# A hybrid of state space, mLSTM and differential attention on one core: one gate laid out turned, products with zeros and unread ones left out, GpSimd's order in the chunk loop, and the weight columns in one transfer

## The reference

```python
h = rmsnorm(x) * ab_norm_g
proj = h @ ab_w_in[i]            # z_a, xbc, dt_raw, z_b, q, k, v, ig, fg, og
y_a = _ssd(xbc, dt_raw, z_a, ...)        # conv, silu, scan over chunks with a state per group
y_b = _mlstm(q, k, v, ig, fg, og, z_b, ...)   # conv, silu, scan with a memory per head
y = concat([y_a, y_b]) @ ab_w_out[i]
# in _ssd:    y = (y_diag + y_off + xs * d_skip) * silu(z);  return rms(y) * norm_g
# in _mlstm:  h = rms(h * sigmoid(o_raw)) * norm_g;          return h * silu(z)
```

## Time and profile before

| | |
|---|---|
| median of 3 runs | 1576.92 us (1575.18 to 1577.39) |
| the profiled execution, its own time | 1573.38 us |
| its span | 1571.6 us |
| TensorE busy | 1525.6 us (97%) |
| VectorE busy | 907.6 us (58%) |
| ScalarE busy | 649.0 us (41%) |
| GpSimd busy | 566.1 us (36%) |
| mean granted clock of TensorE | 0.992 |

### The profile page before, as it was taken

One profiled execution on the slowest core, in us unless ns is written; L12 is line 12 of the kernel. 1 busy time (PEld: TensorE's weight loads), 2 busy tenths in 40 slices (PEclk: granted clock), 3 DMA queues, 4 the chain that ended last, 5 costly groups with the idle time before them and its releaser, 6 DMA issues.

```text
span 1571.6 us, 23657 instructions
## 1 busy us (share of the span) xinstructions
PE 1525.6 (97%) x9114; PEld 1314.0 (84%) x9114; DVE 907.6 (58%) x1484; ACT 649.0 (41%) x1272; POOL 566.1 (36%) x325
## 2 busy tenths in 40 slices
PE   8999999999999999999999999999999999999897
PEld 7798989898999987877788877888888888787686
DVE  7675878684843469999344272345544245554623
ACT  6542534353532233444345252345555333556321
POOL 3245454545344346567565330132212013211110
PEclk9999999999999999999999999999999999999899
DMA  5133333333334345765675330122111112113612
GB/s 178 41 122 94 122 94 121 94 121 94 121 108 135 100 160 186 227 199 175 220 267 201 121 94 14 28 61 76 53 54 34 34 28 80 54 35 114 254 67 107
DMA packets 151085, 176.43 MB, mean 112 GB/s; under 512 B 9671, under 2 KB 126659, under 8 KB 149955
## 3 DMA queue, kind: packets, MB, share of 16 engines
q1 hardware_dynamic: 150810, 174.92, 34.2%
q10 hardware_dynamic: 168, 0.06, 0.0%
HBM read 122.46 MB, written 52.43 MB: 111 GB/s over the span
## 4 chain that ended last, share of the span: by engine, by line
PE 47%; DVE 1%; ACT 1%; issue 1%; DMA 1%; POOL 0%; SPq 0%; POOLq 0%; ACTq 0%; DVEq 0%
PE b_ps L2404 22%; PE b_ps L2449 4%; PE b_ps L2424 4%; PE b_ps L2354 3%; PE b_ps L2356 3%; PE b_ps L2355 3%; PE b_ps L2436 2%; PE b_ps L2506 2%; PE b_ps L2507 2%; PE b_ps L2508 2%; PE b_ps L2457 1%; PE b_ps L2372 0%; DMA b_yy<-z 0%; DMA z<-b_y_T 0%; ACT a_aT L2056 0%
## 5 line engine op out<-in xcount | busy, mean ns | idle before, releaser
L1925 POOL TENSOR_TENSOR b_w<-b_w_raw,b_w 128x1024 fp32r<-128x1024 f32 x66 | 158.4, 2400 | 357.5 <-DVE b_w L2184 253.6
L2404 PE MATMUL b_ps<-a_h_hi,b_w 128*128 128x512 f32 x768 | 265.7, 406 | 2.9 <-DVE a_h_lo L2162 2.9
L393 POOL TENSOR_TENSOR b_w<-b_y_T,b_w 128x1024 fp32r<-128x1024 f32 x54 | 141.1, 2615 | 189.7 <-ACT b_w L451 189.7
L2404 PEld LDWEIGHTS b_ps<-a_h_hi,b_w 128*128 128x128 f32 x768 | 145.0, 189 | 37.1 <-issue 3.9
L2404 PE MATMUL b_ps<-a_h_lo,b_w 128*128 128x512 f32 x384 | 150.6, 392 | 0.0
L941 PE MATMUL b_ps<-b_w,p_hi 128*128 128x256 f32 x768 | 139.2, 283 | 0.0
L700 DVE SCALAR_TENSOR_TENSOR b_w_raw<-p_out_raw,p_cols,b_w_raw 128x1024 f32<-128x1024 f32 x60 | 119.8, 2003 | 12.8 <-ACT b_w_raw L482 11.4
L941 PEld LDWEIGHTS b_ps<-b_w,p_hi 128*128 128x128 f32 x768 | 120.1, 192 | 0.6
L941 PE MATMUL b_ps<-b_w,p_lo 128*128 128x256 f32 x384 | 108.7, 283 | 0.0
L2195 DVE CUSTOM_DVE_ANT_0 b_y_T<-b_ps,a_neg_dist 128x128 f32<-128x128 f32 (+5 forms) x96 | 72.1, 777 | 63.3 <-PE b_ps L2424 52.7
L451 ACT CAST b_w<-b_y_T 128x1024 fp32r<-128x1024 f32 x60 | 62.7, 1045 | 106.5 <-DVE b_y_T L661 55.0
(11 more groups left out here) (417 smaller groups left out, 3616.6 us busy)
## 6 DMA issues: line engine op xcount, KB each, us to landing
b_y_T<-in_ab_w_in SPq DMA_DIRECT2D x33, 512.0 KB, 4.3
tok<-p_out_raw SPq DMA_DIRECT2D x64, 256.0 KB, 2.3
b_w_raw<-in_ab_w_out SPq DMA_DIRECT2D x32, 512.0 KB, 3.7
b_w_raw<-in_c_w_in SPq DMA_DIRECT2D x32, 512.0 KB, 4.1
feat<-b_w_raw SPq DMA_DIRECT2D x20, 512.0 KB, 2.7
c_fe<-feat SPq DMA_DIRECT2D x7, 1280.0 KB, 6.6
yt<-b_y_T SPq DMA_DIRECT2D x8, 1024.0 KB, 10.9
b_y_raw<-yt SPq DMA_DIRECT2D x32, 256.0 KB, 3.9
```

The costliest lines, as they stand in the source:

```text
L393: gp.tensor_tensor(w_lo[s % SLOTS][:, :, :], operand(n, split_of(n, p))[:, :, :], w_hi[s % SLOTS][:, :, :].bitcast(F32), ALU.subtract).the ...
L1925: gp.tensor_tensor(w_lo[:, w, :], w_raw[u % W_RAW][:, :], w_hi[:, w, :].bitcast(F32), ALU.subtract).then_inc(S["l_wlo"], 1)
L2404: mm = pe.matmul(o, x, y, start=(k == 0 and q == 0), stop=(k == KT - 1 and q == 2))
```

## The change

- **Gate turned.** The two token blocks that make z_b (blocks 5 and 7) are computed like feature blocks and stored as features x tokens in a new tensor `zt0`; tok0 has three parts left. After the silu ScalarE multiplies by the norm's gains of the mLSTM. In the scan a chunk's cells of this gate come with a transfer of their own (`load_gate_cells`), and VectorE's copy of the turned y_b multiplies by them. What is left of L1628, the multiplication by the root, goes to ScalarE (`memory_norm`) ahead of the decays.
- **Zeros.** Chunk 0 has no products with the memory and state, no `qs` and no decay of the state; what was added to zeros is copied. The memsets of state and memory go.
- **Unread.** Chunk 7 forms no new memory and state, nor what serves them alone (`xe`, `kg`, keys turned, the state's decay).
- **Order.** `e_end` goes from VectorE to GpSimd; GpSimd's power for y_b goes ahead of its two operations on y_a; next tables ahead of the memory update; waits are split by head and by bank. In the last chunk the splits for the mid products come earlier, on GpSimd and on VectorE, which takes the low parts of units 2 and 3.
- **Columns.** The small vectors come as one matrix `columns` of 128 partitions x 140, laid out by the host (a reordering, and d_skip repeated over the partitions). The transposes and copies of rows at the start of the projection and of the scan go.
- In the projection `sum_weights(n, "T4")` moves ahead of two steps of VectorE.

```diff
-                if kinds[n] == "f":
+                if kinds[n] == "f" or gate_turned(n):
...
+            def gains_of_quarter(n, i, k):
+                if not gate_turned(n):
+                    return
+                c0 = tok_blocks[number[n]][3]
+                for b in (0, 1):
+                    gained[0] += 1
+                    act.wait_ge(S["silu_z"], gained[0])
+                    gain = CELL_GAIN + c0 + 2 * k + b
+                    nc.scalar.activation(area(i, k, b), area(i, k, b), ACT.Copy, scale=cols[:, gain:gain + 1]
+                                         ).then_inc(S["a_out"], 1)
...
+                    if kinds[n] == "t" and k == 2:
+                        gains_of_quarter(n, 0, 0)
+                    if after(n, "t") and k < 3:
+                        gains_of_quarter(n - 1, *((1, 1), (1, 0), (0, 1))[k])
...
-            at = 0
-            for r in rows:
-                act.dma_start(row_in[at:at + r.shape[0], :], r).then_inc(S["rows_in"], 16)
-                at += r.shape[0]
+            act.dma_start(cols[:, :], columns).then_inc(S["cols_in"], 16)
...
                 quarters(n, C11)
+                sum_weights(n, "T4")
                 turned(2)
                 quarters(n, U2)
-                sum_weights(n, "T4")
...
+def load_gate_cells(sp, chunk, n, into, landed):
+    sp.dma_start(into.rearrange("p (f t) -> p f t", t=P), chunk["zt"][:, :, bass.ds(n * P, P)].rearrange("f p t -> p f t")
+                 ).then_inc(landed, 16)
...
                 sp.wait_ge(S["p_cmem"], n + 1)
-                sp.wait_ge(S["d_yb"], n + 1)
                 sp.wait_ge(S["l_yz"], n + 1)
                 load_chunk(sp, chunk, feat, tok, n + 2, par)
                 if behind_first(n):
                     store_y(n - 1, 1 - par)
+                sp.wait_ge(S["d_yT"], n * 4 + 2)
+                load_gate_cells(sp, chunk, n + 2, gz[par][:, 2, :], in_landed[par])
...
                     pe.wait_ge(S["sel_ok"], n + 1)
-                    pe.wait_ge(S["d_cmem"], n * 4)
+                    pe.wait_ge(S["d_cmem"], n * 4 - 3)
                     decays(n, par, 0)
+                    pe.wait_ge(S["d_cmem"], n * 4 - 2)
                     decays(n, par, 1)
...
+                    for k in range(4):
+                        mm = pe.matmul(ps[:, 7, k * P:(k + 1) * P], kt[:, k, :], f[:, QT + k, :], start=True, stop=True)
+                    mm.then_inc(S["p_qk"], 1)
...
-                pe.wait_ge(in_landed[par], prior * 32 + 32)
+                pe.wait_ge(in_landed[par], prior * 48 + 48)
+                pe.wait_ge(S["a_wm"], n + 1)
                 pe.wait_ge(S["d_st"], n + 1)
-                pe.wait_ge(S["d_qs"], n + 1)
-                pe.wait_ge(S["d_cdec"], n + 1)
-                pe.wait_ge(S["a_wm"], n + 1)
-                pe.wait_ge(S["d_cmem"], n * 4)
-
-                pe.wait_ge(S["a_dec"], n * 4 + 4)
-                for h in range(ML_HEADS):
-                    pe.matmul(ps[:, 4 + h, 0:VW], st[:, h, :], va[par][:, h, :], start=True, stop=False)
-                    mm = pe.matmul(ps[:, 4 + h, 0:VW], qs[:, h, :], cmem[:, h, :], start=False, stop=True)
+                if behind_first(n):
+                    pe.wait_ge(S["d_qs"], n + 0)
+                    pe.wait_ge(S["d_cmem"], n * 4)
+
+                for h in (2, 3, 0, 1):
+                    if h == 3 and behind_first(n) and not is_last(n):
+                        pe.wait_ge(S["d_cdec"], n + 0)
+                    if h < 2:
+                        pe.wait_ge(S["a_dec"], n * 4 + 3 + h)
+                    mm = pe.matmul(ps[:, 4 + h, 0:VW], st[:, h, :], va[par][:, h, :], start=True, stop=not behind_first(n))
+                    if behind_first(n):
+                        mm = pe.matmul(ps[:, 4 + h, 0:VW], qs[:, h, :], cmem[:, h, :], start=False, stop=True)
                     mm.then_inc(S["p_num"], 1)
...
+                if is_last(n):
+                    return
                 for h in range(ML_HEADS):
                     pe.wait_ge(S["d_h"], n * 4 + (h + 1))
...
+            def memory_norm(n):
+                act.wait_ge(S["l_rstdm"], n + 1)
+                for h in range(ML_HEADS):
+                    yb = y[:, D + h * ML_V:D + (h + 1) * ML_V]
+                    a = nc.scalar.activation(yb, yb, ACT.Copy, scale=rms[:, 2 + h:3 + h])
+                a.then_inc(S["a_yb"], 1)
...
-            decays(0, (0, 1, 2))
+            decays(0, (0,))
             memory_weights(0)
-            decays(0, (3,))
+            decays(0, (1, 2, 3))
...
                 memory_squares(n)
-                decays(n + 1, (0, 1))
+                memory_norm(n)
+                decays(n + 1, (0, 1, 2))
+                memory_weights(n + 1)
                 ssd_squares(n)
-                decays(n + 1, (2,))
-                memory_weights(n + 1)
                 decays(n + 1, (3,))
                 ssd_norm(n)
...
-                gp.wait_ge(S["a_dec"], n * 4 + 4)
-                gp.tensor_tensor(hd(xe[:, :]), hd(xdt[:, :]),
-                                 dec[:, :, P - 1:P].broadcast_to([P, SSD_HEADS, SSD_DIM]), ALU.mult).then_inc(S["l_xe"], 1)
-                gp.wait_ge(S["p_yoff"], n * 2 + 2)
-                gp.wait_ge(S["d_eend"], n + 1)
-                gp.wait_ge(S["d_state"], n * 2)
-                gp.tensor_tensor(hd(state[:, :]), hd(state[:, :]), last(e_end[:, :], SSD_DIM), ALU.mult).then_inc(S["l_sdec"], 1)
+                if not is_last(n):
+                    gp.wait_ge(S["a_dec"], n * 4 + 4)
+                    gp.tensor_tensor(hd(xe[:, :]), hd(xdt[:, :]),
+                                     dec[:, :, P - 1:P].broadcast_to([P, SSD_HEADS, SSD_DIM]), ALU.mult).then_inc(S["l_xe"], 1)
+                if behind_first(n) and not is_last(n):
+                    if not isinstance(n, int) or n > 1:
+                        gp.wait_ge(S["l_sdec"], n - 1)
+                    gp.tensor_tensor(e_end[:, :], dec[:, :, P - 1:P].rearrange("p h a -> p (h a)"),
+                                     g[:, T_EACS:T_EACS + SSD_HEADS], ALU.mult).then_inc(S["l_eend"], 1)
+                    gp.wait_ge(S["l_eend"], n + 0)
+                    gp.wait_ge(S["p_yoff"], n * 2)
+                    gp.wait_ge(S["d_state"], n * 2)
+                    gp.tensor_tensor(hd(state[:, :]), hd(state[:, :]), last(e_end[:, :], SSD_DIM), ALU.mult).then_inc(S["l_sdec"], 1)
                 spare(0)
                 spare(1)
+                gp.wait_ge(S["d_meanm"], n + 1)
+                gp.tensor_tensor(rms[:, 2:6], rms[:, 2:6], half[:, 0:4], ALU.pow).then_inc(S["l_rstdm"], 1)
                 gp.wait_ge(S["d_y"], n * 2 + 2)
                 gp.wait_ge(S["l_xd"], n + 1)
                 gp.tensor_tensor(y[:, 0:D], y[:, 0:D], x_tok[:, :], ALU.add).then_inc(S["l_yd"], 1)
-                gp.wait_ge(S["d_meanm"], n + 1)
-                gp.tensor_tensor(rms[:, 2:6], rms[:, 2:6], half[:, 0:4], ALU.pow).then_inc(S["l_rstdm"], 1)
                 gp.wait_ge(S["l_yd"], n + 1)
                 if behind_first(n):
-                    gp.wait_ge(in_landed[par], prior * 32 + 32)
+                    gp.wait_ge(in_landed[par], prior * 48 + 48)
                 else:
                     gp.wait_ge(chunk["gate_landed"], 16)
                 gp.tensor_tensor(y[:, 0:D], y[:, 0:D], gates(n, par, 0), ALU.mult).then_inc(S["l_yz"], 1)
-                spare(2)
                 gp.wait_ge(S["d_meany"], n + 1)
...
             def turn(n, part, par, prior=0):
...
+                    by = last(gcols[:, 4 * b:4 * b + 4], P) if part else gate_cells(n, par)[:, 4 * b - 8:4 * b - 4, :]
+                    dve.tensor_tensor(y_T[par][:, 4 * b:4 * b + 4, :], b4(i), by, ALU.mult).then_inc(S["d_yT"], 1)
...
+                if is_last(n):
+                    low_y(0)
+                    low_y(1)
+                    return
...
+                if not is_last(n):
+                    next_tables()
+                    dve.wait_ge(S["p_cmem"], n + 1)
...
-                dve.wait_ge(S["l_rstdm"], n + 1)
-                for h in range(ML_HEADS):
-                    v = slice(h * ML_V, (h + 1) * ML_V)
-                    yb = y[:, D + h * ML_V:D + (h + 1) * ML_V]
-                    a = dve.scalar_tensor_tensor(out=yb, in0=yb, scalar=rms[:, 2 + h:3 + h], in1=gates(n, par, 1)[:, v],
-                                                 op0=ALU.mult, op1=ALU.mult)
-                a.then_inc(S["d_yb"], 1)
```

More of the change, by code:

```diff
@@ L145, with projection_ab @@
 T_USED, T_ALL = 56, 64
-def projection_ab(nc, keep, ahead, x, w_in, rows, feat_cols, feat_out, tok_blocks, tok_out, vectors, load_first, chunk):
-    nrows = sum(r.shape[0] for r in rows)
+def projection_ab(nc, keep, ahead, x, w_in, columns, feat_cols, feat_out, tok_blocks, turned_out, vectors, load_first, chunk):
     nf, nt = len(feat_cols), len(tok_blocks)
@@ L1285, in outputs @@
                 pe.wait_ge(S["d_state"], n * 2)
-                for k in range(2):
+                for k in range(2) if behind_first(n) else ():
```

(5 more changed lines are left out.)

245 lines of the change are left out of this document (129 added, 116 removed).

## The result

| | before | after |
|---|---|---|
| median (range) | 1576.63 us (1575.18 to 1577.39) | 1555.36 us (1552.38 to 1556.27) |
| profiled execution, its time and span | 1573.38, 1571.6 us | 1556.27, 1554.6 us |

The ratio is 0.9863, 95% interval 0.9848 to 0.9878: 21.6 us less, 19 to 24. The profiled executions differ by 17.1 us; the one of before lies 3.3 us under its median, the one of after is the slowest of its four.

A forecast was written before the change was run, and what follows sets the result against it. TensorE was taken to bound the projection, TensorE and VectorE together the chunk loop. Gains of 0.75 + 4.5 + 5.3 + 6.3 + 2.6 = 19.45 us give 1553.9 us for the profiled execution, 1557.5 as a median; range 1553 to 1564.

The forecast's parts named there:

- the likeliest case: Whole kernel: all five parts gain as computed, 19.45 us less, 1557.5 us as a median; chance 0.60.
- its sign: Start of layer 2: forecast wrong if it is not 19 us earlier, or if it is and ends at the same time.
- Step 1: Projection, blocks 5 and 7: products with 512 columns instead of 256 take 0.32 us less each, 2 x 7 products, -4.5 us.
- E: Projection: the turned blocks bring nothing because something other than TensorE paces them; 1562.0 us, chance 0.03.
- Step 2: Kernel start: with columns in one transfer the first transposes no longer wait for rows of gains; -0.75 us.
- Step 3: Chunk 0: numerators start 1.3 us earlier and products with empty memory and state go; -5.3 us, range -3.3 to -5.5.
- rival C: Chunk 0: the clock is down over the numerators, so 1.8 us less is gained; 1559.3 us, chance 0.07.
- Step 4: Loop, chunks 1 to 6: VectorE is relieved and TensorE's 20.95 us of work becomes the bound; -6.3 us (0 to -6.9).
- A: Loop: stays at 22 us a chunk because the denominator's steps wait for GpSimd; 1563.3 us, chance 0.15.
- D: Loop: slower, late GpSimd power delays y's scaling and the next decays; 1581.3 us at 5 us late, chance 0.03.
- Step 5: Chunk 7 to the next stage: unread products go, TensorE stands 3 us for VectorE's turn, stage begins at +12.8; -2.6 us.
- B: Chunk 7: no standing, both low_y fall into a gap of GpSimd; 2.7 us more gained, 1554.8 us, chance 0.10.

The follow-up runs named there:

- e1: The changed kernel with the two gate blocks' products done with 256 columns again, 48 matmuls a product instead of 24; 1561.83 us, ratio 0.9909 to the kernel before.
- e9: The changed kernel with chunk 7's other order, and ScalarE taking the third high parts ahead of chunk 7's scaling of y; 1550.58 us, ratio 0.9838 to before.
- e7: The changed kernel with the next chunk's tables computed after the memory update again; 1565.13 us, ratio 0.9935 to the kernel before.

## Why the prediction came out right, step by step

- **The whole.** 19.45 us were forecast; the profiled pair shows 17.1, the medians 21.3. The mechanisms of the likeliest case are found, but in its sum errors went against each other, which is luck: 4.2 us of gains too little (place 2.6, loop 1.2, chunk 0's entry 0.4), and 5.4 too much (form 1.1, clock 2.0 in chunk 0 and 2.3 in the mid products), with 1.1 more in layer 2, which is scatter. Layer 2 begins 18.1 us earlier (744.77 for 762.90), not the 19 that the prediction set as its sign; by that sign it is just missed.
- **Step 1, gate turned.** The mechanism is right (E falls with e1). The size is 3.4 and not 4.5, 0.24 a product; the 0.32 was read off one pair of rows. At before's place of the operands seven products of either form differ by 2.20 us (40.31 and 38.11), which bears the 0.32 out there, at the new place by 1.17. "Columns in one transfer" also moved the large tensors of the projection by 576 bytes, which no step spoke of: -2.6.
- **Step 2, start.** -0.76 for -0.75; the first transposes start at 7.39 us (7.4 forecast).
- **Step 3, chunk 0.** Numerators 8.46 us after the decays (8.8 forecast), 16.8 us to chunk 1 where fillers kept the clock up (16.75 forecast). In the profiled execution it was down: rival C, priced at 1.8 us on the numerators alone, costs 2.2 there and up to 6 in e9, since the clock can stay down over diagonal and memory products too. It stood at 0.07 and came in six of eight profiles. The forecast had both pauses and the 0.50 of the earlier trace rows before it and gave them too little weight. (Its 7.64 us of dense work are 7.67 by its rows, and the 9.7 us of part 5 are 9.8; neither matters.)
- **Step 4, loop.** 20.77 us a chunk for 21.05: TensorE is the bound, as computed, A and D fall. Of the cover, ScalarE's four scalings take 1.71 us (1.3 forecast) and `e_end` 0.23 (0.7). The steps of the denominator do stand (0.92 us in each chunk), but inside VectorE's slack. I had taken the tables ahead of the memory for a small help; e7 shows that they carry 1.6 us a chunk.
- **Step 5, chunk 7.** +12.4 for +12.8, by another road. Forecast: both `low_y` stand and the diagonal waits 3 us. Found: `low_y(0)` fell into a gap, the diagonal waited 0.93, and the two denominator steps stood 0.8 and 2.1 us for GpSimd's low parts, so the first mid product waited 1.39. B, in which neither `low_y` stands, falls with `low_y(1)`, which took 1.54 us. That the clock could be down behind a pause at that place, as in four of six profiles, was not in the working at all.

## To carry to other kernels

Before a stage with dense matmuls, a pause of TensorE can cost twice: itself, and, in part of the profiles here, the clock behind it; look at the granted clock of the stretch behind each new pause, and see whether the last operations in front can be reordered before filling the pause. Small VectorE operations with SBUF inputs stood beside GpSimd's long products and not beside its power, so place them by what GpSimd does then: move the whole group, since half of such a move can be slower than none. When a change adds or removes a small tensor, see which large ones move in SBUF, and price one part of the change in a kernel that has the same addresses.

## What was not expected of the hardware

- The pace of TensorE's products changes with the place in SBUF of tensors that hold part of their operands: the same projection takes 535.8, 537.1 or 540.4 us with the tensors behind the columns 0, 128 or 64 bytes on, and the kernel before 541.6 or 539.0 us with 0 or 576. The Trainium skill (SBUF — State Buffer, Who interferes with whom) gives TensorE two read ports of its own, independent of each other, and says that it waits on nobody; TensorE shows no waits here either, yet its matmuls follow each other at another pace. What in the address decides was not found.
- A VectorE copy of 56 columns takes 0.19 us beside a GpSimd power and 1.29 beside a GpSimd addition.
- Of the versions, the fastest that is clear of the changed kernel is the changed kernel with chunk 7's other order, 1550.29 us, ratio 0.9833 to before. With fillers as well it is 1549.33 us at 0.9842: the two can't be told apart.
